# A head's output with tokens on partitions, and attention weights left unnormalised, in a two-layer hybrid decoder trunk

## Chip, cores and metric

One Trainium2 chip, one core, one launch. The metric is the device time of the kernel in microseconds (us). Everything is computed to float32 accuracy: where a matrix product is large, each float32 operand is split into a high and a low part and three products are summed (high x high, high x low, low x high).

## The reference

Two layers over x of 512 tokens by 1024 channels. A layer is a SwiGLU block, a token mixing block and a second SwiGLU block, each behind an RMSNorm with shift, scale and gate from a vector c. The mixing block projects to q, k, v, to the input u of a convolution branch and to two gates. Of its attention branch this matters here:

```
s = einsum('bqhmd,bkhmd->bhmqk', q, k) * scale + bias       # 8 heads, 2 maps (m) each
p = softmax(where(dist >= 0, s, neg))
w = p[:, :, 0] - lam * p[:, :, 1]
o = einsum('bhqk,bkhe->bqhe', w, v)                         # e = 128
o = rms_norm(o, subln_gain) * (1 - lam_init)                # over the 128 channels of a head
y_attn = o.reshape(B, S, 1024) @ w_attn_branch
```

The convolution branch is a gated input (`glu` below), a causal depthwise convolution of width 31, a LayerNorm over channels and a product with a matrix. Since rms_norm divides by sqrt(mean(o^2) + eps), a row of o that is r times too large has the same norm if eps is multiplied by r^2. That identity is what the change uses.

## The kernel before, in words

Activations lie with channels on partitions and the 512 tokens in the free dimension. Every large product is cut into slabs: a weight slab is 1024 x 128, that is 8 blocks of 128x128 (k = 0 to 7). For each slab four steps follow one another. SP loads it (`w_raw`), ACT rounds it to the high part (`w_hi`, `w_hi_part`, L377), DVE subtracts to get the low part (`w_lo`, `w_lo_part`, L605), and PE runs 24 matmuls of 128x512 on it (L1045 to L1047, `slab`). There are two slots of each buffer; the slabs alternate between them, so the `w_hi` of a slab waits until PE has finished the slab two before it, and DVE's `w_lo` waits for that `w_hi`.

The order of every engine is written out by hand; nothing schedules it. In the mixing block one function `mix` per engine handles a head; the first head is written out, the other seven are a loop. A head has six slabs, called slab 0 to 5 here, for q, k, v, the two halves of u, and gate a. The attention work of a head is spread over its own slabs 3 to 5 and over slabs 0 to 2 of the next head:

- PE puts small pieces into slabs by a table `at={k: ...}` (before block k). The scores of the four query blocks (L1222) come at k = 4 of slab 3, behind slab 3, at k = 4 of slab 4 and of slab 5. The weights are turned by transposes (L1198). In the next head, `values` (L1205) follows at k = 4 of slab 1 and `head_mean` (L1210, the mean of the squares over partitions as a product with a constant matrix, L1072) at k = 3 of slab 2.
- DVE interleaves with its `w_lo` parts the 31 taps of the previous head's convolution (`conv`, L858, 0.75 us each), the row maxima (`scores`, L890, and the sign change, L893) and `combine` (L901 to L908), which makes of two exponentials the difference of two softmaxes. It ends a head with `glu` (L944), from which the next 31 taps start. In slabs 1 and 2 of the next head it takes the reciprocal of the root, 128x512 (L616), multiplies o by gain and reciprocal (L627), and later subtracts for `ao_lo` (L634).
- ACT copies results from PSUM, makes the `w_hi` parts and the exponentials (L511), and for the previous head copies o (`head_output`, L499), squares it (L500), takes the root (L384, its table loaded ahead at L381) and rounds the product to `ao_hi` (L396).

Here o comes out of PE with its 128 channels on partitions, so its norm is a sum over partitions, and root and reciprocal stand repeated on all 128 partitions as 128x512.

Behind the loop come gate b (`gb`, four pairs of slabs), the attention projection (`ab`), the convolution projection and the output projection. The last head's rest and 31 taps fall into `gb`; PE's mean over the convolution's sum (L1272) waits for the last tap.

The neighbouring pieces of DVE's program in a head, which the steps of the prediction follow:

```
conv(8, 17)
w_lo_part(p + 1, 1)
if not first:
    reciprocal(...)
    unit_gain(uh, 0, True, OT[:, :], subg[:, ds(l, 1)])
w_lo_part(p + 2, 0)
conv(17, 19)
```

Here `p` counts pairs of slabs: `w_lo_part(p + 1, 1)` is slab 3, `w_lo_part(p + 2, 0)` slab 4, and `w_lo_part(p + 3, 0)` slab 0 of the next head.

Of the kernel before, what the change touches and what calls it, by code (L numbers as in the profile page):

```python
# [27 lines left out]
P = 128  # L28
# [47 lines left out]
AUXN = 3 + HEADS + 2  # L76
AUX_NORM = (0, 1, AUXN - 1)
AUX_HEAD, AUX_MEAN, AUX_VAR = 2, 2 + HEADS, 3 + HEADS

RSN = 3 + HEADS + 1  # L80
RS_NORM = (0, 1, RSN - 1)
RS_HEAD, RS_VAR = 2, 2 + HEADS

UNITS = 3 * KT + HEADS + KT
UNIT_NORM = (0, KT, UNITS - KT)
UNIT_HEAD, UNIT_LN = 2 * KT, 2 * KT + HEADS
# [34 lines left out]
def build(nc, a, onehot, out):  # L121
# [86 lines left out]
    OT = at("o_t", [P, TOK], F32, mr0)  # L208
# [163 lines left out]
    def _(act):  # L372
# [93 lines left out]
        with act.Fori(0, DEPTH) as l:  # L466
            for w in range(2):
# [29 lines left out]
                def head_output(hh):  # L497
                    act.wait_ge(sem("o_ready"), hh + 1)
                    act.activation(OT[:, :], O[:, :], ACT.Copy).then_inc(sem("o_copied"), 1)  # L499
                    act.activation(SQ[:, :], O[:, :], ACT.Square).then_inc(sem("o_read"), 1)  # L500

                def mix(h, first):
# [49 lines left out]
                for j in range(KT):  # L552
# [13 lines left out]
                    if j == 0:  # L566
                        unit_hi(l * UNITS + UNIT_HEAD + HEADS - 1, 0, AOHI[:, HEADS - 1, :])
# [33 lines left out]
    def _(dve):  # L601
# [154 lines left out]
        with dve.Fori(0, DEPTH) as l:  # L756
            for w in range(2):
# [113 lines left out]

                def mix(h, first):
# [3 lines left out]
                    uh = l * UNITS + UNIT_HEAD + h - 1  # L876
# [18 lines left out]
                    def combine(i):  # L895
# [26 lines left out]
                    if not first:  # L922
                        unit_lo(uh, 0, tile(AOLO2, h - 1), tile(AOHI2, h - 1))
# [13 lines left out]
                    combine(0)  # L937
                    if not first:
# [14 lines left out]
                for j in range(KT):  # L953
# [12 lines left out]
                    if j == 0:  # L966
                        uh = l * UNITS + UNIT_HEAD + HEADS - 1
# [360 lines left out]
```

## Time and profile before

| what | value |
|---|---|
| median of 3 runs | 2756.42 us (2755.35 to 2757.57) |
| the profiled execution | 2755.38 us |
| its span, first to last instruction | 2753.7 us |
| mean granted clock of TensorE | 0.978 |
| busy: PE, DVE, ACT | 94%, 63%, 39% of the span |
| traffic with HBM | 319.6 MB, 116 GB/s over the span |

The page gives busy shares over the whole span. Which engine sets the pace of a stage is read from the busy time by stretch and from what each engine waited for in it. A duration in the trace is that of one instruction from start to end; instructions of one engine overlap a little at their ends, so the distance from start to start is the time that one takes in a row of many. "Idle before" is the time from the modelled end of the instruction ahead. The granted clock is 1.00 at 2.4 GHz and 0.50 at 1.2 GHz.

### The profile page before, as it was taken

Reading aid. Unit: us, or ns where it says so; the run is one execution under the profiler, and the core shown is the slowest. Engines: PE = TensorE matmul, PEld = TensorE weight load, DVE = VectorE, ACT = ScalarE, POOL = GpSimd, SP = SyncE. Lnnn points to the kernel's source line nnn. Section 1 sums busy time; section 2 is a strip of 40 time slices with the busy share of each in tenths; the row PEclk is TensorE's granted clock in tenths of the full one; section 3 lists DMA queues with packets and bytes.
Section 4 is the critical chain, followed back from the end, with each engine's and each line's share of the span. In section 5 each row is a group of like instructions: output and inputs, shape, how many; then the busy total and the mean of one; then the engine's idle time right before and its main releaser. Section 6 shows DMA issues by size and latency. Waiting matters only on the chain.

```text
span 2753.7 us, 35127 instructions
## 1 busy us (share of the span) xinstructions
PE 2585.2 (94%) x11186; PEld 2030.9 (74%) x11186; DVE 1748.2 (63%) x2545; ACT 1060.4 (39%) x1497; POOL 81.7 (3%) x162
## 2 busy tenths in 40 slices
PE   4899998999999989999979999989999999899997
PEld 2688886776767767888858888867766678688886
DVE  3655567799998555543345556669999965655433
ACT  2433322444443434343234342244444443443422
POOL 0000010000000000000000001100000000000000
PEclk9999998999999999999989999989999999999998
DMA  5444474222222233433324446622222223343332
GB/s 221 142 149 142 151 224 142 81 76 72 80 80 84 84 114 115 152 122 95 97 83 145 153 129 208 211 66 79 76 73 83 77 87 122 101 143 107 97 92 93
DMA packets 472262, 320.39 MB, mean 116 GB/s; under 512 B 11303, under 2 KB 447785, under 8 KB 471176
## 3 DMA queue, kind: packets, MB, share of 16 engines
q1 hardware_dynamic: 445260, 227.69, 28.1%
q0 software_dynamic: 21888, 83.90, 8.9%
q10 hardware_dynamic: 5052, 8.02, 1.0%
q8 instruction: 33, 0.54, 0.1%
q14 instruction: 29, 0.24, 0.0%
HBM read 314.52 MB, written 5.05 MB: 116 GB/s over the span
## 4 chain that ended last, share of the span: by engine, by line
PE 68%; DVE 16%; issue 11%; ACT 3%; ACTq 1%; DVEq 1%
PE bank L1045 21%; PE bank L1047 21%; PE bank L1046 21%; DVE conv_part L858 5%; DVE rstd L616 3%; DVE w_lo L605 2%; ACTq L420 1%; ACT w_hi L377 1%; DVE probs L890 1%; PE bank L1063 1%; PE bank L1064 1%; PE bank L1065 1%; PE bank L1100 1%; DVE probs L906 1%; PE bank L1127 1%
## 5 line engine op out<-in xcount | busy, mean ns | idle before, releaser
L605 DVE TENSOR_TENSOR w_lo<-w_raw,w_hi 128x1024 fp32r<-128x1024 f32 (+1 forms) x434 | 522.6, 1205 | 721.5 <-ACT w_hi L377 720.6
L1046 PE MATMUL bank<-h_lo,w_hi 128*128 128x512 f32 x2336 | 911.3, 390 | 0.0
L1045 PE MATMUL bank<-h_hi,w_hi 128*128 128x512 f32 x2208 | 885.9, 401 | 17.9 <-DVE w_lo L605 17.8
L1047 PE MATMUL bank<-h_hi,w_lo 128*128 128x512 f32 x2208 | 862.9, 391 | 0.0
L377 ACT ACTIVATE w_hi<-w_raw 128x1024 fp32r<-128x1024 f32 (+1 forms) x434 | 452.4, 1043 | 912.8 <-PE bank L1047 893.1
L1045 PEld LDWEIGHTS bank<-h_hi,w_hi 128*128 128x128 f32 x2208 | 415.5, 188 | 134.9 <-issue 52.2
L1046 PEld LDWEIGHTS bank<-h_lo,w_hi 128*128 128x128 f32 x2336 | 440.1, 188 | 89.9 <-issue 3.8
L1047 PEld LDWEIGHTS bank<-h_hi,w_lo 128*128 128x128 f32 x2208 | 415.4, 188 | 89.0
L858 DVE SCALAR_TENSOR_TENSOR conv_part<-glu,conv_taps,conv_part 128x512 f32<-128x512 f32 x464 | 316.6, 747 | 0.0
L1045 PE MATMUL bank<-s_hi,w_hi 128*128 128x512 f32 x704 | 274.9, 390 | 0.0
L1047 PE MATMUL bank<-s_hi,w_lo 128*128 128x512 f32 x704 | 274.0, 389 | 0.0
L1046 PE MATMUL bank<-s_lo,w_hi 128*128 128x512 f32 x704 | 273.9, 389 | 0.0
L673 DVE SCALAR_TENSOR_TENSOR ada_acc<-ada_raw,c_act,ada_acc 128x1024 f32<-128x1024 f32 x126 | 161.2, 1280 | 0.6
L1045 PEld LDWEIGHTS bank<-s_hi,w_hi 128*128 128x128 f32 x704 | 132.1, 188 | 27.7
L1047 PEld LDWEIGHTS bank<-s_hi,w_lo 128*128 128x128 f32 x704 | 132.1, 188 | 27.6
L1046 PEld LDWEIGHTS bank<-s_lo,w_hi 128*128 128x128 f32 x704 | 132.2, 188 | 27.4
L353 POOL DMA_DIRECT2D ada_raw<-in_ada_w x144 | 76.3, 530 | 2401.5 <-DVE scaled L1006 1065.0
L478 ACT ACTIVATE s_hi<-full 128x512 f32 x88 | 55.7, 633 | 175.0 <-DVE full L779 175.0
L511 ACT ACTIVATE probs<-probs,neg_row_max 128x512 f32<-128x512 f32 (+3 forms) x128 | 71.0, 556 | 115.0 <-DVE neg_row_max L893 114.9
L377 ACT ACT_TABLE_LOAD x88 | 112.9, 1283 | 1.6
L781 DVE TENSOR_TENSOR s_lo<-full,s_hi 128x512 f32 (+1 forms) x88 | 61.0, 693 | 80.3 <-ACT s_hi L478 80.3
L616 DVE RECIPROCAL rstd<-rstd 128x512 f32<-128x512 f32 x25 | 83.7, 3350 | 13.8 <-ACT rstd L384 13.8
(158 smaller groups left out, 2296.5 us busy)
## 6 DMA issues: line engine op xcount, KB each, us to landing
w_raw<-in_ffn_w_in SPq DMA_DIRECT2D x176, 512.0 KB, 3.8
ada_raw<-in_ada_w POOLq DMA_DIRECT2D x144, 512.0 KB, 4.7
w_raw<-in_w_mix_in SPq DMA_DIRECT2D x112, 512.0 KB, 3.7
w_raw<-in_ffn_w_out SPq DMA_DIRECT2D x64, 512.0 KB, 3.6
w_raw<-in_ffn_w_out SPq DMA_DIRECT2D x32, 384.0 KB, 3.1
w_raw<-in_w_mix_out SPq DMA_DIRECT2D x18, 512.0 KB, 3.6
ada_first<-in_ada_w POOLq DMA_DIRECT2D x8, 1024.0 KB, 24.4
w_raw<-in_w_attn_branch SPq DMA_DIRECT2D x16, 512.0 KB, 3.6
```

The costliest lines, as they stand in the source:

```text
L353: pool.dma_start(ada_raw[k % 4][:, :], w_ada[:, ds(layer * KT + k, 1), ds(m * D, D)].rearrange("p o f -> p (o f)"))\
L377: act.activation(whi[slot][:, 0:n, :], raw[slot][:, 0:n, :], ACT.Copy).then_inc(w_hi[slot], 1)
L478: act.activation(tile(SHI2, i), F[0][:, :], ACT.Copy).then_inc(sem("s_hi"), 1)
L511: act.activation(PR[par][m][:, 0:n], PR[par][m][:, 0:n], ACT.Exp, bias=nmx[:, par, m:m + 1], accum_out=rsum[:, par, m:m + 1]).then_inc(sem ...
L605: dve.tensor_tensor(wlo[slot][:, 0:n, :], raw[slot][:, 0:n, :], whi[slot][:, 0:n, :].bitcast(F32), ALU.subtract).then_inc(w_lo[slot], 1)
L616: dve.reciprocal(RSTD[:, :], RSTD[:, :]).then_inc(sem("rstd_ready"), 1)
L673: ins = dve.scalar_tensor_tensor(out=ACC[:, :], in0=ada_raw[k % 4][:, :], scalar=CA[:, k:k + 1], in1=ACC[:, :], op0=ALU.mult, op1=ALU.add)
L781: dve.tensor_tensor(tile(SLO2, i), F[0][:, :], tile(SHI2, i).bitcast(F32), ALU.subtract)\
L858: ins = dve.scalar_tensor_tensor(out=CAB[t % 2][:, :], in0=Z[:, t:t + TOK], scalar=wt, in1=CAB[t % 2][:, :], op0=ALU.mult, op1=ALU.add)
L1045: pe.matmul(acc, wh, hi[:, k0 + k, :], start=first and k == 0, stop=False)
L1046: pe.matmul(acc, wh, lo[:, k0 + k, :], start=False, stop=False)
L1047: mm = pe.matmul(acc, wl, hi[:, k0 + k, :], start=False, stop=last and k == n - 1)
```

## The change

The output of a head is made with tokens on partitions: ten matmuls of 128x128 with the turned weights as the stationary operand, where there were four with V stationary. The sum of squares of a token is then a row sum, which ACT's square gives along with it, and root and reciprocal are 128x4. Four copies with that reciprocal as the scale make the normalised rows, four transposes on PE (`turn_o`) bring the channels back to partitions, and ACT and DVE make `ao_hi` and `ao_lo` from the result with the gain.

The weights are left unnormalised: `combine` forms e0 - lam * (s0 / s1) * e1 (s0, s1 the row sums of the two maps), which is s0 times the former weights. The norm takes this factor out again, with eps * s0^2 as the bias of the root. On DVE the scaling of the second map by its reciprocal (L906) is thus gone.

Places: PE's `head_mean` at k = 3 of slab 2 goes, `turn_o` comes at k = 6 of slab 2. On DVE the small reciprocal stands where the large one stood. On ACT `head_root` stands where `head_output` stood, ahead of the `w_hi` of slab 3, and `head_rows` where `root` stood, ahead of the `w_hi` of slab 4. For the last head `turn_o` comes at k = 2 of slab 0 of gate block 1.

The diff, without tables of counts, declarations and waits of DVE on its own small results (`sum_eps` is called behind `combine(0)`, `head_lo` where `unit_lo` was):

```diff
 ACT
-                def head_output(hh):
+                def head_root(hh):
                     act.wait_ge(sem("o_ready"), hh + 1)
-                    act.activation(OT[:, :], O[:, :], ACT.Copy).then_inc(sem("o_copied"), 1)
-                    act.activation(SQ[:, :], O[:, :], ACT.Square).then_inc(sem("o_read"), 1)
+                    for i in range(QB):
+                        act.activation(SQ[:, i * P:(i + 1) * P], O[:, i * P:(i + 1) * P], ACT.Square,
+                                       accum_out=oss[:, i:i + 1]).then_inc(sem("o_squared"), 1)
+                    act.wait_ge(sem("o_squared"), (hh + 1) * QB)
+                    act.wait_ge(sem("head_eps"), hh + 1)
+                    for i in range(QB):
+                        act.activation(ort[:, i:i + 1], oss[:, i:i + 1], ACT.Sqrt, bias=head_eps[:, i:i + 1],
+                                       scale=1.0 / P).then_inc(sem("o_root"), 1)
+                def head_rows(hh):
+                    act.wait_ge(sem("o_inv"), hh + 1)
+                    act.wait_ge(sem("ot_ready"), hh)
+                    for i in range(QB):
+                        act.activation(OS[:, i * P:(i + 1) * P], O[:, i * P:(i + 1) * P], ACT.Copy,
+                                       scale=ori[:, i:i + 1]).then_inc(sem("o_read"), 1)
+                def head_hi(hh, h):
+                    act.wait_ge(sem("ot_ready"), hh + 1)
+                    act.activation(tile(AOHI2, h), AUX[:, :], ACT.Copy, scale=subg[:, ds(l, 1)]).then_inc(sem("ao_hi"), 1)
...
-                        head_output(hh - 1)
+                        head_root(hh - 1)
                     w_hi_part(p + 1, 1)
                     act.activation(KTT[:, :], G[1][:, :], ACT.Copy).then_inc(acc_read[1], 1)
                     if not first:
-                        root(l * AUXN + AUX_HEAD + h - 1, l * UNITS + UNIT_HEAD + h - 1, float(D // P))
+                        head_rows(hh - 1)
                     w_hi_part(p + 2, 0)
                     act.activation(VT[:, :], G[0][:, :], ACT.Copy).then_inc(acc_read[0], 1)
                     if not first:
-                        unit_hi(l * UNITS + UNIT_HEAD + h - 1, 0, tile(AOHI2, h - 1))
+                        head_hi(hh - 1, h - 1)
 DVE
+                def head_inverse(hh):
+                    dve.wait_ge(sem("o_root"), (hh + 1) * QB)
+                    dve.wait_ge(sem("o_read"), hh * QB)
+                    dve.reciprocal(ori[:, :], ort[:, :]).then_inc(sem("o_inv"), 1)
+                def head_lo(hh, h):
+                    dve.wait_ge(sem("ao_hi"), hh + 1)
+                    dve.scalar_tensor_tensor(out=tile(AOLO2, h), in0=AUX[:, :], scalar=subg[:, ds(l, 1)],
+                                             in1=tile(AOHI2, h).bitcast(F32), op0=ALU.mult, op1=ALU.subtract)
...
-                        dve.reciprocal(rinv[:, par, :], rsum[:, par, :]).then_inc(sem("comb"), 1)
-                        dve.tensor_scalar(rlam[:, par:par + 1], rinv[:, par, 1:2], nlam[:, ds(l, 1)], None, ALU.mult)
-                        dve.tensor_scalar(p1, p1, rlam[:, par:par + 1], None, ALU.mult).then_inc(sem("comb"), 1)
-                        dve.scalar_tensor_tensor(out=p0, in0=p0, scalar=rinv[:, par, 0:1], in1=p1,
+                        dve.reciprocal(rinv[:, i:i + 1], rsum[:, i, 1:2]).then_inc(sem("comb"), 1)
+                        dve.scalar_tensor_tensor(out=ratio[:, i:i + 1], in0=rsum[:, i, 0:1], scalar=nlam[:, ds(l, 1)],
+                                                 in1=rinv[:, i:i + 1], op0=ALU.mult, op1=ALU.mult)
+                        dve.scalar_tensor_tensor(out=p0, in0=p1, scalar=ratio[:, i:i + 1], in1=p0,
                                                  op0=ALU.mult, op1=ALU.add).then_inc(sem("w_ready"), 1)
+                    def sum_eps():
+                        dve.wait_ge(sem("o_root"), hh * QB)
+                        dve.scalar_tensor_tensor(out=head_eps[:, :], in0=rsum[:, :, 0], scalar=EPS, in1=rsum[:, :, 0],
+                                                 op0=ALU.mult, op1=ALU.mult).then_inc(sem("head_eps"), 1)
...
-                        reciprocal(l * AUXN + AUX_HEAD + h - 1, l * RSN + RS_HEAD + h - 1)
-                        unit_gain(uh, 0, True, OT[:, :], subg[:, ds(l, 1)])
+                        head_inverse(hh - 1)
 PE
-                    for j in range(QB):
-                        mm = pe.matmul(O[:, j * P:TOK], V[:, j, :], WT[:, j, j * P:TOK], start=(j == 0), stop=(j == QB - 1))
+                    for i in range(QB):
+                        for j in range(i + 1):
+                            mm = pe.matmul(O[:, i * P:(i + 1) * P], WT[:, j, i * P:(i + 1) * P], V[:, j, :],
+                                           start=(j == 0), stop=(j == i))
...
+                def turn_o(hh):
+                    pe.wait_ge(sem("o_read"), (hh + 1) * QB)
+                    pe.wait_ge(sem("ao_lo"), hh)
+                    for i in range(QB):
+                        mm = pe.transpose(AUX[:, i * P:(i + 1) * P], OS[:, i * P:(i + 1) * P], ident[:, :])
...
-                    slab(p + 1, 0, G[0][:, :], HHI, HLO, at={} if first else {3: lambda: head_mean(h - 1)})
+                    slab(p + 1, 0, G[0][:, :], HHI, HLO, at={} if first else {6: lambda: turn_o(hh - 1)})
...
-                head_mean(HEADS - 1)
+                branch("gb", 1, HHI, HLO, ({2: lambda: turn_o(last)}, {}))
```

How the order of instructions moves, at two places. ACT, inside the head loop, from the turned weights of query block 0 to the first exponential's table; `w_hi_55` is slab 3, `w_hi_54` slab 4. Before:

```order
L493 ACTIVATE weights_t<-bank 128x128
L499 ACTIVATE o_t<-bank 128x512
L500 ACTIVATE squares<-bank 128x512
L377 ACTIVATE w_hi_55<-w_raw_53 128x1024
L522 ACTIVATE k_t<-bank 128x512
L381 ACT_TABLE_LOAD
L381 ACTIVATE root_warm<-eps 128x1
L382 REGISTER_ALU
L383 ISA
L384 ACTIVATE rstd<-bank,eps 128x512
L375 ISA
L377 ACTIVATE w_hi_54<-w_raw_52 128x1024
```

And after the change (L381 is now `w_hi`):

```order
L497 ACTIVATE weights_t<-bank 128x128
L505 ACTIVATE squares,o_square_sum<-bank 128x128 x4
L507 REGISTER_ALU
L510 ACT_TABLE_LOAD
L510 ACTIVATE o_root<-o_square_sum,head_eps 128x1 x4
L381 ACTIVATE w_hi_55<-w_raw_53 128x1024
L546 ACTIVATE k_t<-bank 128x512
L518 ACTIVATE o_rows<-bank,o_root_inv 128x128 x4
L379 ISA
L381 ACTIVATE w_hi_54<-w_raw_52 128x1024
```

The root and its table load have moved ahead of the `w_hi` of slab 3; ahead of the `w_hi` of slab 4 stand the copies that need the reciprocal.

DVE, inside the head loop, from the last of nine taps over `w_lo` of slab 3 to the next two taps. Before:

```order
L605 TENSOR_TENSOR w_lo_57<-w_raw_53,w_hi_55 128x1024
L615 REGISTER_ALU
L616 RECIPROCAL rstd<-rstd 128x512
L617 REGISTER_ALU
L626 ISA
L627 REGISTER_ALU
L627 SCALAR_TENSOR_TENSOR scaled_61<-o_t,subln,rstd 128x512
L604 REGISTER_ALU
L605 TENSOR_TENSOR w_lo_56<-w_raw_52,w_hi_54 128x1024
```

And after the change (L630 is now `w_lo`):

```order
L630 TENSOR_TENSOR w_lo_57<-w_raw_53,w_hi_55 128x1024
L899 ISA
L900 ISA
L901 RECIPROCAL o_root_inv<-o_root 128x4
L629 REGISTER_ALU
L630 TENSOR_TENSOR w_lo_56<-w_raw_52,w_hi_54 128x1024
```

The reciprocal keeps its place between the two `w_lo`, at a 128th of the size, and the multiplication behind it is gone.

## Rows read from the trace of the kernel before

**Rows 1.** The page: the span, and busy time, share and instructions of each engine.
```profile
span 2753.7 us, 35127 instructions
...
PE 2585.2 (94%) x11186; PEld 2030.9 (74%) x11186; DVE 1748.2 (63%) x2545; ACT 1060.4 (39%) x1497; POOL 81.7 (3%) x162
```

**Rows 2.** Busy time by stretch (us and instructions, clock, DMA share, GB/s), one head.
```profile
564.40:608.80 44.40, 42.27 (x185) 30.67 (x184) 42.46 (x84) 20.88 (x40) 0.00 (x0) 1.00 0.27 77
```

**Rows 3.** Timeline of DVE, same head: start us, us, engine, line, operation [idle before].
```profile
562.86 0.69 DVE L944 SCALAR_TENSOR_TENSOR glu<-full,scaled 128x512 f32<-128x512 f32 x1
...
569.86 6.05 DVE L858 SCALAR_TENSOR_TENSOR conv_part<-glu,conv_taps,conv_part 128x512 f32<-128x512 f32 x9
575.83 1.22 DVE L605 TENSOR_TENSOR w_lo<-w_raw,w_hi 128x1024 fp32r<-128x1024 f32 x1
576.96 3.35 DVE L616 RECIPROCAL rstd<-rstd 128x512 f32<-128x512 f32 x1
580.54 0.75 DVE L627 SCALAR_TENSOR_TENSOR scaled<-o_t,subln,rstd 128x512 f32<-128x512 f32 x1 [0.23 <-DVE rstd L616]
581.21 1.22 DVE L605 TENSOR_TENSOR w_lo<-w_raw,w_hi 128x1024 fp32r<-128x1024 f32 x1
...
597.44 1.23 DVE L605 TENSOR_TENSOR w_lo<-w_raw,w_hi 128x1024 fp32r<-128x1024 f32 x1 [0.69 <-ACT w_hi L377]
...
607.33 0.69 DVE L944 SCALAR_TENSOR_TENSOR glu<-full,scaled 128x512 f32<-128x512 f32 x1
```

**Rows 4.** Timeline of PE in the same head, columns as in rows 3.
```profile
570.09 0.47 PE L1045 MATMUL bank<-h_hi,w_hi 128*128 128x512 f32 x1 [0.39 <-DVE w_lo L605]
...
572.25 1.02 PE L1072 MATMUL bank<-squares,inv_d 128*128 128x512 f32 x2
...
573.34 0.39 PE L1046 MATMUL bank<-h_lo,w_hi 128*128 128x512 f32 x1
...
576.33 0.39 PE L1047 MATMUL bank<-h_hi,w_lo 128*128 128x512 f32 x1
...
577.19 0.47 PE L1045 MATMUL bank<-h_hi,w_hi 128*128 128x512 f32 x1 [0.48 <-DVE w_lo L605]
...
585.25 0.92 PE L1222 MATMUL bank<-k_t,q_t 64*128 64x384 f32 x4 [1.03 <-DVE neg_row_max L893]
...
586.09 0.66 PE L1230 MATMUL bank<-ident,v_t 128*128 128x128 f32 x4
...
586.82 0.39 PE L1046 MATMUL bank<-h_lo,w_hi 128*128 128x512 f32 x1
```

**Rows 5.** Groups of instructions over the whole span: count, busy us, mean ns.
```profile
L906 DVE TENSOR_SCALAR probs<-probs,row_inv_lam 128x512 f32<-128x512 f32 (+1 forms) x64 | 24.8, 387 | 2.2
...
L901 DVE RECIPROCAL row_inv<-row_sum 128x2 f32<-128x2 f32 x64 | 10.1, 159 | 0.0
...
L493 ACT ACTIVATE weights_t<-bank 128x128 f32<-128x128 f32 x16 | 4.3, 268 | 0.0
```

**Rows 6.** Timeline of ACT in the same head, columns as in rows 3.
```profile
571.36 1.28 ACT L381 ACT_TABLE_LOAD   x1
...
576.81 1.06 ACT L377 ACTIVATE w_hi<-w_raw 128x1024 fp32r<-128x1024 f32 x1 [2.73 <-PE bank L1047]
```

**Rows 7.** Two idle stretches of PE (timeline), and the clock behind each (by stretch).
```profile
866.12 1.12 PE L1072 MATMUL bank<-running_sum,inv_d 128*128 128x512 f32 x2 [1.79 <-DVE running_sum L870]
...
904.27 0.47 PE L1045 MATMUL bank<-ao_hi,w_hi 128*128 128x512 f32 x1 [3.18 <-DVE gate_a L960]
...
866.20:869.50 3.30, 3.27 (x12) 2.08 (x13) 3.21 (x5) 0.60 (x1) 0.00 (x0) 1.00 0.29 88
...
905.60:908.90 3.30, 3.30 (x10) 2.53 (x9) 1.96 (x4) 2.44 (x4) 0.00 (x0) 0.50 0.82 245
```

**Rows 8.** Timeline of DVE behind the head loop, columns as in rows 3.
```profile
829.64 0.69 DVE L944 SCALAR_TENSOR_TENSOR glu<-full,scaled 128x512 f32<-128x512 f32 x1
...
838.91 1.23 DVE L605 TENSOR_TENSOR w_lo<-w_raw,w_hi 128x1024 fp32r<-128x1024 f32 x1 [4.60 <-ACT w_hi L377]
```

More of the change, by code:

```diff
@@ L73 @@
 USE0, USES = starts(PH_USES)
-AUXN = 3 + HEADS + 2
+AUXN = 5
 AUX_NORM = (0, 1, AUXN - 1)
-AUX_HEAD, AUX_MEAN, AUX_VAR = 2, 2 + HEADS, 3 + HEADS
-RSN = 3 + HEADS + 1
+AUX_MEAN, AUX_VAR = 2, 3
+RSN = 4
 RS_NORM = (0, 1, RSN - 1)
-RS_HEAD, RS_VAR = 2, 2 + HEADS
-UNITS = 3 * KT + HEADS + KT
+RS_VAR = 2
+UNITS = 4 * KT
 UNIT_NORM = (0, KT, UNITS - KT)
-UNIT_HEAD, UNIT_LN = 2 * KT, 2 * KT + HEADS
+UNIT_LN = 2 * KT
 ZERO_FFN1, ZERO_CONV, ZERO_LN, ZERO_MO, ZERO_FFN2, ZEROS = 1, 2, 3, 4, 5, 5
@@ L189, in build @@
     nmx = at("neg_row_max", [P, 2, 2], F32)
-    rsum = at("row_sum", [P, 2, 2], F32)
-    rinv = at("row_inv", [P, 2, 2], F32)
-    rlam = at("row_inv_lam", [P, 2], F32)
+    rsum = at("row_sum", [P, QB, 2], F32)
+    rinv = at("row_inv", [P, QB], F32)
+    ratio = at("row_ratio", [P, QB], F32)
+    head_eps = at("head_eps", [P, QB], F32)
+    oss = at("o_square_sum", [P, QB], F32)
+    ort = at("o_root", [P, QB], F32)
+    ori = at("o_root_inv", [P, QB], F32)
     SHI = at("s_hi", [P, FT, TOK], F32R, r0)
@@ L207, in build @@
     VT = at("v_t", [P, TOK], F32, ph + 4 * KB)
-    OT = at("o_t", [P, TOK], F32, mr0)
+    OS = at("o_rows", [P, TOK], F32, mr0)
     V = at("v", [P, QB, P], F32, ph + 6 * KB)
@@ L560, in _ @@
                         weights(0, l * HEADS + HEADS - 1)
-                        head_output(l * HEADS + HEADS - 1)
-                        root(l * AUXN + AUX_HEAD + HEADS - 1, l * UNITS + UNIT_HEAD + HEADS - 1, float(D // P))
+                        head_root(l * HEADS + HEADS - 1)
                     w_hi_part(p + 1, 1)
@@ L566, in _ @@
                     if j == 0:
-                        unit_hi(l * UNITS + UNIT_HEAD + HEADS - 1, 0, AOHI[:, HEADS - 1, :])
+                        head_rows(l * HEADS + HEADS - 1)
+                    if j == 1:
+                        head_hi(l * HEADS + HEADS - 1, HEADS - 1)
                     if j == LN_MEAN:
@@ L937, in mix @@
                     combine(0)
+                    sum_eps()
                     if not first:
@@ L966, in _ @@
                     if j == 0:
-                        uh = l * UNITS + UNIT_HEAD + HEADS - 1
-                        reciprocal(l * AUXN + AUX_HEAD + HEADS - 1, l * RSN + RS_HEAD + HEADS - 1)
-                        unit_gain(uh, 0, True, OT[:, :], subg[:, ds(l, 1)])
+                        head_inverse(l * HEADS + HEADS - 1)
                         taps(HEADS - 1, 5, 8)
-                        unit_lo(uh, 0, AOLO[:, HEADS - 1, :], AOHI[:, HEADS - 1, :])
                         taps(HEADS - 1, 8, 13)
                     if j == 1:
+                        head_lo(l * HEADS + HEADS - 1, HEADS - 1)
                         taps(HEADS - 1, 22, DVE_TAPS)
@@ L1267, in _ @@
                 branch("gb", 0, HHI, HLO, ({4: lambda: turn_weights(1, last)}, {1: lambda: turn_weights(0, last), 6: lambda: values(last)}))
-                head_mean(HEADS - 1)
-                with pe.Fori(1, LN_MEAN + 1) as i:
+                branch("gb", 1, HHI, HLO, ({2: lambda: turn_o(last)}, {}))
+                with pe.Fori(2, LN_MEAN + 1) as i:
                     branch("gb", i, HHI, HLO)
                 pe.wait_ge(sem("csum"), (l + 1) * KT)
+                pe.wait_ge(sem("ao_lo"), (l + 1) * HEADS)
                 mean(l * AUXN + AUX_MEAN, SSUM[:, :])
@@ L1275, in _ @@
                 with pe.Fori(0, LN_VAR + 1 - KT // 2) as i:
-                    pe.wait_ge(sem("unit_lo"), l * UNITS + UNIT_HEAD + HEADS)
+                    pe.wait_ge(sem("ao_lo"), (l + 1) * HEADS)
                     branch("ab", i, AOHI, AOLO)
```

23 lines of the change are left out of this document (10 added, 13 removed).

## The prediction

> **What bounds the kernel now.** I read the page, then the busy time by stretch, then the timelines of VectorE (DVE), TensorE (PE) and ScalarE (ACT) through one head. The page shows PE busy 94% of the span and DVE 63% [rows 1]. The share is an average over stages. In the head loop, the only stage that the change touches besides the block behind it, DVE is busy 42.46 of 44.40 us and PE 42.27, ACT only 20.88 [rows 2]. From one `glu` to the next is 44.47 us [rows 3]. DVE's idle in it is the 0.69 us shown and some 0.35 behind `glu`. PE, in contrast, has real waits, and all are for DVE: 0.39, 0.48 and 1.03 us of idle [rows 4]. An idle figure counts from the modelled end of a 0.39 us matmul, while matmuls start every 0.23 us (13 starts in the 2.99 us from 573.34 to 576.33 [rows 4]), so each hides 0.16 us more. With two smaller waits that makes 2.8 us, and PE's own work in a head is 41.7 us. DVE sets the period; PE is 2.8 us behind it. A DVE that is faster gives at most 2.8 us a head, unless something new is late.
>
> **What DVE loses and gains per head.** The reciprocal of 128x512 and the wait behind it go, from 576.96 to 580.54: 3.58 us. So does the multiplication by gain and rstd, from 580.54 to 581.21: 0.67 [rows 3]. The four scalings of `probs` go: 4 x 0.387 = 1.55 us [rows 5]. The 128x2 reciprocals and the little product behind them keep their number. Added are a reciprocal of 128x4 and one 128x4 product for `head_eps`; the nearest row is the 128x2 reciprocal, 0.16 each [rows 5]; bounds 0.1 and 0.25, I take 0.16. `ao_lo` stays one 128x512 operation. Net: 3.58 + 0.67 + 1.55 - 0.32 = 5.5 us less work a head, nearly twice what PE could follow.
>
> **Where the new wait is.** Before, the mean of squares was taken at k = 3 of slab 2, and nothing in PE's order waited for DVE's reciprocal. Now PE's `turn_o`, at k = 6 of slab 2, waits for ACT's `head_rows`, and that waits for DVE's `head_inverse`. The latter has kept its place, behind 17 taps and two `w_lo`. Behind the waiting PE instruction are the last six matmuls of slab 2; behind those ACT's `w_hi` of slab 4; behind that DVE's very next instruction, `w_lo` of slab 4. It is a ring. Call the start of the small reciprocal R.
> - Reciprocal 0.16, hand-over 0.05.
> - ACT, four copies of 128x128. One such copy is 0.27 us [rows 5]. One behind another they would be 1.07, and if they overlap by a tenth as long ones do, 0.75. I take 0.8. PE can start at R + 1.05.
> - PE, four transposes. From 586.09 to 586.82 are four transposes and one matmul: 0.73 - 0.23 = 0.50 [rows 4]. Then six matmuls, 1.38, and 0.16 for the tail of the last: R + 3.1.
> - ACT, `w_hi`: it started at 576.81, 0.48 us behind the start of the last matmul (576.33), and took 1.06 [rows 4, 6]. R + 4.25.
>
> DVE, ready at R + 0.2, idles 4.1 us, where before `w_lo` came at once [rows 3]. Two smaller waits follow. `scores(3)` needs PE's slab 3 up to k = 4: R + 1.05, 0.50 and 18 matmuls 4.1, then two score matmuls, 1.2 (the narrower pair at 585.25 took 0.84 [rows 4], times 4/3, and a tail): R + 6.9. DVE is there after `w_lo` 1.13 and two taps (nine take 5.97 us, from 569.86 to 575.83 [rows 3]): R + 6.7. With the hand-over 0.3 us. `w_lo` at 597.44 waited for ACT, which waits for the maxima ahead of `combine(2)`, so what that combine saves, 0.4 us, is lost there. The period is 44.47 - 5.5 + 4.1 + 0.3 + 0.4 = 43.8 us: 0.7 less, over the seven `glu` intervals of a layer 4.9, for two layers **9.8 us less**.
>
> PE's work changes too: mean out, 1.09 - 0.23 = 0.86 (572.25 to 573.34 [rows 4]); transposes in, 0.50; the values in ten matmuls for four, of the same 1280 columns, which I put at 0.1 (bounds 0 and 0.5). That is 41.4 us, so PE waits some 2.4 us at `turn_o`, 2.2 us as the profile counts idle. ACT gains four squares, four roots and four copies. The table load of 1.28 us [rows 6] stood behind `k_t` and ahead of its wait; now it stands behind the squares, ahead of `w_hi` of slab 3. Between the values and `turn_o` lie 30 matmuls, 6.9 us, and the stall, so the values are there at R - 8.2. Squares 1.4 (four at the copy's 0.27 and a tenth more for the sum), load 1.28, roots 0.8, `w_hi` 1.06 and hand-overs 0.2 end at R - 3.5. DVE wants that `w_hi` at R - 1.1: nothing waits, and the cover is 2.4 us.
>
> **What the stall does to PE's clock.** Idle of 1.79 us before 866.12 left the granted clock at 1.00; 3.18 us before 904.27 were followed by 3.3 us at 0.50, that is 1.2 GHz in place of 2.4 [rows 7]. The new stall, 2.2 us, lies between and recurs in every head. In such a stretch PE does 3.3 us of work in twice the time, so loses 1.7 us, and it loses them just where DVE waits for PE (the 0.3 us before `scores(3)`). The cost of a fall is between 0 (where DVE has slack) and 1.7; I take 1.3, near the upper end because the ring lies there. For the number of falls I have only the two rows, so take the middle: half, 7 of 14. That is **+9 us**. The Trainium skill (TensorE: Matmul & The Clock Gate, "HAM oscillation — how this bites in real kernels") describes a loop whose waits let the clock fall again in each pass; by it every head would pay. Its section "What's actually happening" lets the clock fall only after an idle stretch; by that a stall this short would cost nothing. The first is rival B's time, the second rival A's.
>
> **Behind the loop.** Before, from `glu` at 829.64 to the mean at 866.12 are 36.5 us, all DVE, with 4.60 us idle before `w_lo` at 838.91 [rows 7, 8]. Reciprocal and gain go there too, 4.2. But PE now comes later relative to DVE, so DVE idles about 1.1 us more before the first `w_lo` and 1.2 before the second (root and table load ahead of it). `turn_o` in slab 0 of gate block 1 stalls PE 4.4 us, which delays the `w_hi` of block 2 by 1.9. Sum 0. That stall is beyond the 3.18 us, so the clock falls, on this ring: +1.3 a layer, **+2.6 us**. Head 0 and everything else are unchanged.
>
> **Sum.** -9.8 + 9 + 2.6 = +1.8 us on the profiled execution's 2755.38 (span 2753.7 and 1.7 around it), which is 1.0 under the median of the runs. On the median: 2756.4 + 1.8 = 2758. A measurement of this kernel can tell about 0.2%, 5.5 us, from no change.
>
> **Rivals.**
> - A, the clock holds (chance 0.2): the ring as above without falls in the loop. -9.8 + 2.6 = -7: 2749. For it: 2.2 us is nearer to 1.79 than to 3.18.
> - B, slower (0.25): the clock falls in every head, at the full 1.7 us. -9.8 + 14 x 1.7 + 2.6 = +17: 2773. At 1.3 a fall it is +11. It decides from a stall just over 1.79 us, or from copies that cost their upper bound, 0.3 us more a head, 4 us in all.
> - C, no ring (0.05): DVE's relief goes through and PE sets the period, 41.4 us. 14 x 3.1 = 43 us less: 2713. Against it: the order on DVE puts the reciprocal 14 us behind `glu`, and PE is at `turn_o` before that.
> - D, ACT is late (0.05): squares with their sums and the roots cost over 2.4 us more than I count, and `w_hi` of slab 3 holds DVE ahead of the reciprocal. Each further us costs 14: about 2770.
>
> **How the numbers follow.** The forecast, a gain of the loop given back through the clock, has 0.45: 2758, its own range 2751 to 2765. The range over the cases reaches down past A with copies at their lower bound and up to B at the middle of its prices: 2745 to 2771. Faster by over 0.2%: most of A and all of C, 0.25. Slower: B, D and the upper edge of the forecast, 0.32. Within: 0.43.
>
> **What would show it.** In the new profile `turn_o` should be PE's longest wait in a head, 2 to 3 us, released by `o_rows`; the other PE waits in the head nearly gone; DVE idle some 4 us before the `w_lo` behind the 128x4 reciprocal, released by `w_hi`; a `glu` period of 43.8 us where the clock is full and about 45 where it fell. Intervals near 41.4 us would refute the ring. Intervals of 43.8 throughout would be A, of 45 or more throughout B. A wait of DVE before `w_lo` of slab 3 would be D.

## The result, and the profile after

| | this kernel | kernel before |
|---|---|---|
| median | 2781.39 us (2777.96 to 2782.35, 4 runs) | 2756.99 us (2755.35 to 2757.99, 4 runs) |
| profiled execution, its span | 2777.96, 2776.2 us | 2755.38, 2753.7 us |
| mean granted clock | 0.970 | 0.978 |

The ratio is 1.0087, 95% interval 1.0071 to 1.0103: slower by 24 us, where 2758 (2745 to 2771) was forecast. The profiled execution was the fastest of the four and is 22.5 us longer in its span than that of before.

The page answers to [rows 1]: DVE is busy for 81 us less, PE for nearly the same (2.3 us more).

```profile
span 2776.2 us, 35599 instructions
...
PE 2587.5 (93%) x11410; PEld 2062.8 (74%) x11410; DVE 1667.3 (60%) x2481; ACT 1077.8 (39%) x1689; POOL 81.4 (3%) x162
```

Busy time by stretch (as [rows 2]), two heads from one `glu` to the next:

```profile
609.00:653.50 44.50, 41.05 (x200) 31.73 (x199) 37.44 (x80) 21.96 (x52) 0.00 (x0) 1.00 0.26 76
653.50:699.70 46.20, 42.75 (x201) 32.92 (x199) 37.50 (x81) 21.98 (x52) 0.00 (x0) 0.96 0.26 74
```

In the first the clock was full: 44.5 us, DVE busy for 37.44 where it was 42.46. The head is no shorter. In the second the granted clock was 0.96 on average and the head took 46.18 us, 1.6 us more.

DVE's timeline in the first of these heads answers to [rows 3]; the bracket is the idle before and what ended it:

```profile
608.96 0.69 DVE L985 SCALAR_TENSOR_TENSOR glu<-full,scaled 128x512 f32<-128x512 f32 x1
...
621.92 1.23 DVE L630 TENSOR_TENSOR w_lo<-w_raw,w_hi 128x1024 fp32r<-128x1024 f32 x1
623.06 0.18 DVE L901 RECIPROCAL o_root_inv<-o_root 128x4 f32<-128x4 f32 x1
627.70 1.23 DVE L630 TENSOR_TENSOR w_lo<-w_raw,w_hi 128x1024 fp32r<-128x1024 f32 x1 [4.46 <-ACT w_hi L381]
...
630.36 0.69 DVE L927 CUSTOM_DVE_ANT_0 probs<-bank,bias_tile 128x512 f32<-128x512 f32 x1
...
643.66 1.23 DVE L630 TENSOR_TENSOR w_lo<-w_raw,w_hi 128x1024 fp32r<-128x1024 f32 x1 [1.14 <-ACT w_hi L381]
...
646.68 0.06 DVE L925 MEMSET spare<- 128x1 f32 x1 [0.47 <-PE bank L1237]
...
653.51 0.69 DVE L985 SCALAR_TENSOR_TENSOR glu<-full,scaled 128x512 f32<-128x512 f32 x1
```

The large reciprocal (3.35 us) has become 0.18 us, and the `w_lo` behind it, which used to come at once, waits 4.46 us. Two waits stand later in the head: 1.14 us before the `w_lo` of slab 0 (0.69 before), and 0.47 us ahead of `scores(0)`, for the turned weights, where there was none. Before `scores(3)` there is hardly a wait: its first instruction starts at 630.36, 0.1 us behind the two taps. From `glu` to `glu` are 653.51 - 608.96 = 44.55 us, against 44.47.

ACT and PE at the place of the ring, as [rows 6] and [rows 4]. ACT:

```profile
615.40 1.28 ACT L510 ACT_TABLE_LOAD   x1
616.70 0.85 ACT L510 ACTIVATE o_root<-o_square_sum,head_eps 128x1 f32<-128x1 f32 x4
617.46 1.04 ACT L381 ACTIVATE w_hi<-w_raw 128x1024 fp32r<-128x1024 f32 x1
...
623.27 1.14 ACT L518 ACTIVATE o_rows<-bank,o_root_inv 128x128 f32<-128x128 f32 x4 [4.29 <-DVE o_root_inv L901]
626.60 1.06 ACT L381 ACTIVATE w_hi<-w_raw 128x1024 fp32r<-128x1024 f32 x1 [2.19 <-PE bank L1086]
```

PE, the last matmul before the transposes, the transposes, and a matmul behind them:

```profile
620.63 0.39 PE L1086 MATMUL bank<-h_hi,w_lo 128*128 128x512 f32 x1
624.47 0.66 PE L1254 MATMUL bank<-ident,o_rows 128*128 128x128 f32 x4 [3.45 <-ACT o_rows L518]
...
625.19 0.39 PE L1085 MATMUL bank<-h_lo,w_hi 128*128 128x512 f32 x1
```

Here the ring can be followed. The reciprocal starts at 623.06, the four copies at 623.27 take 1.14 us, PE's transposes start at 624.47 after 3.45 us of idle, the last six matmuls of slab 2 follow, `w_hi` starts at 626.60, and DVE's `w_lo` at 627.70: 4.64 us from the reciprocal, of which DVE worked 0.2. ACT, in contrast, had its `w_hi` of slab 3 done at 618.50, 3.4 us before DVE wanted it: the roots and their table load delayed nothing.

What the stall does to the clock is seen one head earlier. PE:

```profile
578.43 1.11 PE L1254 MATMUL bank<-ident,o_rows 128*128 128x128 f32 x4 [3.45 <-ACT o_rows L518]
579.20 0.78 PE L1084 MATMUL bank<-h_hi,w_hi 128*128 128x512 f32 x1
579.77 0.63 PE L1085 MATMUL bank<-h_lo,w_hi 128*128 128x512 f32 x1
580.20 0.63 PE L1086 MATMUL bank<-h_hi,w_lo 128*128 128x512 f32 x1
```

and the stretch behind the stall:

```profile
578.30:581.50 3.20, 3.07 (x10) 2.59 (x11) 0.00 (x0) 0.08 (x1) 0.00 (x0) 0.50 0.55 164
```

The granted clock was 0.50, and matmuls start every 0.43 us (579.77, 580.20) instead of every 0.23. In that head DVE waits longer for the `w_hi`:

```profile
583.14 1.23 DVE L630 TENSOR_TENSOR w_lo<-w_raw,w_hi 128x1024 fp32r<-128x1024 f32 x1 [5.94 <-ACT w_hi L381]
```

In the loop the clock fell in 11 of 14 heads; those take 45.9 to 46.2 us, the others 44.55. In six of the eleven the low stretch begins up to 0.5 us before the transposes, and this wait is 5.81 to 5.94 us instead of 4.46. In the other five it begins some 1.8 us later; the wait is 4.85 to 4.93 us, and the one before `scores(3)` has grown from 0.1 to 1.26 to 1.32 us.

DVE behind the loop, answering to [rows 8]:

```profile
837.74 0.69 DVE L985 SCALAR_TENSOR_TENSOR glu<-full,scaled 128x512 f32<-128x512 f32 x1
839.02 1.23 DVE L630 TENSOR_TENSOR w_lo<-w_raw,w_hi 128x1024 fp32r<-128x1024 f32 x1 [0.59 <-ACT w_hi L381]
...
848.68 1.22 DVE L630 TENSOR_TENSOR w_lo<-w_raw,w_hi 128x1024 fp32r<-128x1024 f32 x1 [5.60 <-ACT w_hi L381]
...
859.03 1.23 DVE L630 TENSOR_TENSOR w_lo<-w_raw,w_hi 128x1024 fp32r<-128x1024 f32 x1 [3.76 <-ACT w_hi L381]
...
874.81 0.69 DVE L895 TENSOR_TENSOR running_sum<-running_sum,conv 128x512 f32<-128x512 f32 x1
```

The wait for `w_hi` is 5.60 us instead of 4.60, and two others have come, 0.59 and 3.76. They eat what the reciprocal gave. PE's stall at `turn_o` is 4.55 us there, and the clock falls in both layers, for 3.4 and 6.8 us. It fell there in the kernel before as well, for as long, behind a wait of PE for `w_lo`:

```profile
851.55 0.77 PE L1045 MATMUL bank<-h_hi,w_hi 128*128 128x512 f32 x1 [3.54 <-DVE w_lo L605]
```

But from there to the mean DVE waited for no other engine, so that fall did not delay it; now DVE waits for the `w_hi` behind it. The wait of 3.76 us is 4.52 in the other layer, where the clock was low for longer.

**Where the 22.5 us are** (profiled executions, by the starts of `glu` and of the means on PE). The seven intervals of a layer took 311.3 us; now 319.4 and 320.9, together 17.7 more. Without falls they would be 7 x 44.55 = 311.9, so 1.2 us belong to the head as it is at full clock and 16.5 to the clock, 1.5 us for each of the eleven falls. From the last `glu` to the mean 36.5 us have become 37.9 and 38.6 (38.65): 3.6. The rest, 1.2 us, lies elsewhere; its cause was not looked for.

### The profile page after: what moved, and what is told of

Read it like the earlier page. It is cut to its first block, busy times and chain, and to the rows that moved or that the text cites. A ratio compares the mean times of both kernels' runs of the same rounds, so it can differ in the third digit from the quotient of the medians.

```text
span 2776.2 us, 35599 instructions
## 1 busy us (share of the span) xinstructions
PE 2587.5 (93%) x11410; PEld 2062.8 (74%) x11410; DVE 1667.3 (60%) x2481; ACT 1077.8 (39%) x1689; POOL 81.4 (3%) x162
## 4 chain that ended last, share of the span: by engine, by line
PE 80%; DVE 9%; issue 7%; ACT 3%; ACTq 1%; DVEq 1%
PE bank L1084 24%; PE bank L1085 24%; PE bank L1086 24%; DVE conv_part L883 3%; PE bank L1267 2%; DVE w_lo L630 1%; ACTq L424 1%; DVE rstd L641 1%; PE bank L1102 1%; PE bank L1103 1%; PE bank L1104 1%; ACT w_hi L381 1%; PE bank L1139 1%; ACT o_rows L518 1%; PE bank L1254 1%
## 5 line engine op out<-in xcount | busy, mean ns | idle before, releaser
L630 DVE TENSOR_TENSOR w_lo<-w_raw,w_hi 128x1024 fp32r<-128x1024 f32 (+1 forms) x434 | 522.8, 1205 | 815.1 <-ACT w_hi L381 814.2
L1084 PE MATMUL bank<-h_hi,w_hi 128*128 128x512 f32 x2208 | 884.0, 400 | 0.1
L381 ACT ACTIVATE w_hi<-w_raw 128x1024 fp32r<-128x1024 f32 (+1 forms) x434 | 452.1, 1042 | 897.5 <-PE bank L1086 877.8
L1102 PE MATMUL bank<-h_hi,w_hi 128*128 128x512 f32 x96 | 47.9, 499 | 46.7 <-DVE h_lo L661 46.7
```

The source lines that it names most:

```text
L381: act.activation(whi[slot][:, 0:n, :], raw[slot][:, 0:n, :], ACT.Copy).then_inc(w_hi[slot], 1)
L630: dve.tensor_tensor(wlo[slot][:, 0:n, :], raw[slot][:, 0:n, :], whi[slot][:, 0:n, :].bitcast(F32), ALU.subtract).then_inc(w_lo[slot], 1)
L1084: pe.matmul(acc, wh, hi[:, k0 + k, :], start=first and k == 0, stop=False)
L1102: pe.matmul(acc, wh, hi[:, n, :], start=n == 0, stop=False)
```

## The experiments

The theory after this reading: in a head DVE's relief is given back through a ring (reciprocal, copies, `turn_o`, end of slab 2, `w_hi`, `w_lo`), and the PE stall in it makes the clock fall, 1.5 us each time. The rivals: the added instructions cost the time, or the long heads have another cause and the clock only follows.

A block is three matmuls. All medians are beside runs of the kernel before, which gave 2754.65 us in the first four experiments and 2755.88 in the others.

### e1: `turn_o` in slab 3

```diff
-slab(p + 1, 0, ..., at={} if first else {6: lambda: turn_o(hh - 1)})
+slab(p + 1, 0, ...)
-slab(p + 1, 1, ..., at={4: lambda: scores(3)})
+slab(p + 1, 1, ..., at={4: lambda: scores(3)} if first else {3: lambda: turn_o(hh - 1), 4: lambda: scores(3)})
-branch("gb", 1, HHI, HLO, ({2: lambda: turn_o(last)}, {}))
+branch("gb", 1, HHI, HLO, ({}, {3: lambda: turn_o(last)}))
```

> Theory (a ring through PE's wait at turn_o): with turn_o at k = 3 of slab 3 the w_hi and w_lo of slab 4 no longer hang on DVE's reciprocal. DVE's idle of 4.5 us before the w_lo behind it goes; about 2 us come back before scores(3), which needs slab 3 of PE. Period of a head 41.5 to 42.3 us, no fall of the clock in the loop, 2712 to 2725 us. Rival (the added instructions themselves cost the time: ten value matmuls for four, four squares, roots and copies on ACT): nothing is left out here, so it stays within 5 us of 2781.

Measured: 2717.9 us median, ratio 0.9864 (0.9848 to 0.9881). A head takes 42.03 us, the first of a layer 42.70, no fall in the loop. The same instructions in another place are 63 us faster than the change and 37 faster than before. The added work is thus not the cause; the place of one wait is. Of the ring's wait, 4.46 us, this is left (those of 1.14 and 0.47 us later in the head stay):

```profile
661.62 1.23 DVE L630 TENSOR_TENSOR w_lo<-w_raw,w_hi 128x1024 fp32r<-128x1024 f32 x1 [2.16 <-ACT w_hi L381]
```

2.16 us: slab 2 ends later than DVE is ready, but no longer on account of the reciprocal. I had expected the 2 us before `scores(3)`; no wait shows there, so the period came out right with the wait in another place. Behind the loop, where `turn_o` moved too, 34.0 us are left of the 37.9 and 38.6.

### e2: the stall filled

```diff
                 def turn_o(hh):
+                    pe.wait_ge(sem("ao_lo"), hh)
+                    for _ in range(3):
+                        pe.matmul(AUX[:, :], invd[:, :], X[:, 0, :], start=True, stop=True)
                     pe.wait_ge(sem("o_read"), (hh + 1) * QB)
-                    pe.wait_ge(sem("ao_lo"), hh)
```

> The change with three mean-sized matmuls (0.86 us each, results overwritten by the transposes) put into PE's stall before turn_o, so that PE is at work there; the ring stays as it is. Theory (each fall of the clock costs about 1.5 us, eleven in the loop): all heads take 44.5 to 44.7 us, 2781 - 16 = 2763 to 2767 us. Rival (the 46 us heads are long for another reason, and the clock falls in them as a consequence): no gain, 2780 or above, since work was only added.

Measured: 2758.99 us median, ratio 1.0014 (1.0005 to 1.0024), 4 us below the expected range. PE in a head (the three matmuls are six records):

```profile
621.00 2.74 PE L1253 MATMUL bank<-x_res,inv_d 128*128 128x512 f32 x6
624.60 0.66 PE L1256 MATMUL bank<-ident,o_rows 128*128 128x128 f32 x4 [0.86 <-ACT o_rows L518]
```

The filling lasts 2.74 us and 0.86 us of idle are left. No fall in the loop, and twelve of the fourteen intervals are 44.51 to 44.55 us (the first of each layer 45.29, since there the stall was short and the filling costs). Work was added and 22 us went: the falls are the cause of the long heads, not their consequence. The ring is unchanged (DVE waits 4.46 us in it, as in the change), and a head is still 0.05 us longer than one of before, so the kernel is no faster than before either. The profiled executions differ by 16.8 us in span (2759.4): 15.3 in the loop, that is eleven falls at 1.5 less what the filling costs in the two first heads, and 2.0 behind it, where the filling stands too, which I had not counted (elsewhere e2 takes 0.5 more). There one layer had a fall and took 38.06 us, the other had none and took 36.45, as long as before the change. The medians differ by 5.6 us more than the spans, since the profiled execution of the change was 3.4 us under its median and that of e2 2.2 over it.

### e3: the reciprocal earlier

```diff
-                    conv(8, 17)
-                    w_lo_part(p + 1, 1)
+                    conv(8, 12)
                     if not first:
                         head_inverse(hh - 1)
+                    conv(12, 17)
+                    w_lo_part(p + 1, 1)
```

> The small reciprocal moved up by five taps and one w_lo on DVE, everything else as in the change. Theory (ring): the rows are there before PE reaches turn_o at k = 6 of slab 2, no stall, no fall; period 41.3 to 42.2 us, 2710 to 2723 us. If instead ACT's root is not ready so early, DVE waits before the reciprocal, and the gain is halved. Rival (added work): within 5 us of 2781.

Measured: 2723.19 us median, ratio 0.9887 (0.9870 to 0.9903), at the upper end of the expected range. A head takes 41.64 us. The ring is opened at its other end, with nearly the same effect. PE no longer waits at `turn_o`; its one wait of the head is for the low part of slab 3:

```profile
660.40 0.47 PE L1085 MATMUL bank<-h_hi,w_hi 128*128 128x512 f32 x1 [0.51 <-DVE w_lo L630]
```

Behind the loop `turn_o` still stalls for 4.5 us; the two stretches there take 38.0 and 39.2 us against 34.0 in e1. That is why e1, 4.5 us slower in the loop, is faster in all.

### e4: `turn_o` one block later

```diff
-slab(p + 1, 0, ..., at={} if first else {6: lambda: turn_o(hh - 1)})
+slab(p + 1, 0, ..., at={} if first else {7: lambda: turn_o(hh - 1)})
```

> turn_o one block (three matmuls, 0.69 us) later in slab 2. Theory (ring): the ring holds three matmuls of slab 2 instead of six, so a head without a fall takes 44.55 - 0.69 = 43.9 us; PE's stall shrinks to some 3 us but the clock still falls in most heads, at 1.5 us. 14 x 0.69 = 10 us less: 2769 to 2773 us. Rival (the place of turn_o is indifferent, DVE's own work sets the head): 2781.

Measured: 2759.65 us median (2756.76 to 2770.74, 10 runs), ratio 1.0024 (1.0012 to 1.0036). Heads without a fall take 43.84 to 43.87 us, 0.69 less, which is the three matmuls (3 x 0.23). PE's idle in most heads:

```profile
580.64 0.66 PE L1254 MATMUL bank<-ident,o_rows 128*128 128x128 f32 x4 [2.76 <-ACT o_rows L518]
```

The miss is in the number of falls: I expected most heads, and the profiled execution had only 4 in 14. Seven falls fewer than in the change, at 1.5 us, are 10.5 us. They bring the theory's 2771 us down to 2760.5, near the measured time, which is 9 us below the expected range. Only the profiled execution shows its falls; the ten runs lie 14 us apart.

### e5: the weights part alone, on the kernel before

Without waits and counts:

```diff
-                        dve.reciprocal(rinv[:, par, :], rsum[:, par, :])
-                        dve.tensor_scalar(rlam[...], rinv[:, par, 1:2], nlam[:, ds(l, 1)], None, ALU.mult)
-                        dve.tensor_scalar(p1, p1, rlam[:, par:par + 1], None, ALU.mult)
-                        dve.scalar_tensor_tensor(out=p0, in0=p0, scalar=rinv[:, par, 0:1], in1=p1, ...)
+                        dve.reciprocal(rinv[:, par, 1:2], rsum[:, par, 1:2])
+                        dve.scalar_tensor_tensor(out=rlam[...], in0=rsum[:, par, 0:1], scalar=nlam[:, ds(l, 1)],
+                                                 in1=rinv[:, par, 1:2], op0=ALU.mult, op1=ALU.mult)
+                        dve.scalar_tensor_tensor(out=p0, in0=p1, scalar=rlam[:, par:par + 1], in1=p0, ...)
```

> The kernel before with only the weights left unnormalised (the scaling L906 gone); eps of the head's norm is left unscaled. Theory (before, DVE sets the head, and the place ahead of the w_lo of slab 0, where DVE waits for ACT anyway, swallows 0.4 us): 44.47 - 1.7 + 0.4 = 43.1 to 43.4 us a head, 15 to 19 us less than before: 2737 to 2741 us. Rival (PE or ACT carries the head as much as DVE): no change, 2755.

Measured: 2739.27 us median, ratio 0.9943 (0.9927 to 0.9958), a head 43.23 us. This half of the change is a gain of 17 us. DVE:

```profile
604.68 0.68 DVE L942 SCALAR_TENSOR_TENSOR glu<-full,scaled 128x512 f32<-128x512 f32 x1
...
638.72 1.23 DVE L605 TENSOR_TENSOR w_lo<-w_raw,w_hi 128x1024 fp32r<-128x1024 f32 x1 [1.14 <-ACT w_hi L377]
...
647.90 0.68 DVE L942 SCALAR_TENSOR_TENSOR glu<-full,scaled 128x512 f32<-128x512 f32 x1
```

The wait before this `w_lo` has grown from 0.69 to 1.14 us, as in the changed kernel: 0.45 of the saving is swallowed there. PE followed DVE down to 43.23 us, so DVE did set the head before.

### e7: the output part alone

`combine` is as in the kernel before (L901 to L908). Besides:

```diff
-                    act.wait_ge(sem("head_eps"), hh + 1)
...
-                        act.activation(ort[:, i:i + 1], oss[:, i:i + 1], ACT.Sqrt, bias=head_eps[:, i:i + 1],
+                        act.activation(ort[:, i:i + 1], oss[:, i:i + 1], ACT.Sqrt, bias=eps[:, 0:1],
...
-                    sum_eps()
```

> The change with the weights normalised as before (L906 back) and a constant eps: the new head output alone. Theory (DVE's work is part of the ring with the stall): some 1 us of the 1.7 comes on top in each head, 45.4 to 45.7 us without a fall, and PE's longer stall lets the clock fall in nearly all: 2790 to 2800 us. Rival (the ring is made of hand-overs only, DVE's work is beside it): 2781.

Measured: 2801.86 us median, ratio 1.0171 (1.0156 to 1.0187), 2 us above the expected range. Heads are 47.6 to 48.0 us (46.78 once), the first of a layer 45.2, and the clock fell in 12 of 14. This half costs 46 us. DVE in a head with a fall:

```profile
632.80 1.22 DVE L630 TENSOR_TENSOR w_lo<-w_raw,w_hi 128x1024 fp32r<-128x1024 f32 x1 [6.09 <-ACT w_hi L382]
...
636.54 0.69 DVE L927 CUSTOM_DVE_ANT_0 probs<-bank,bias_tile 128x512 f32<-128x512 f32 x1 [1.19 <-issue]
...
650.35 1.23 DVE L630 TENSOR_TENSOR w_lo<-w_raw,w_hi 128x1024 fp32r<-128x1024 f32 x1 [0.69 <-ACT w_hi L382]
```

DVE waits 6.09 us behind the reciprocal, and 1.19 before the scores. I had counted 1.5 us for a fall; here 11 of the 12 low stretches lasted 6.8 us instead of 3.4. What a fall of that length costs is read from e4 and e8, which have heads without one: 2.7 to 2.8 us, against 1.3 to 1.7 for one of 3.4. That a head without a fall would take 45.4 to 45.7 us stays open, as every head but the first of a layer had one.

### e8: one copy for four

```diff
-                    for i in range(QB):
-                        act.activation(OS[:, i * P:(i + 1) * P], O[:, i * P:(i + 1) * P], ACT.Copy,
-                                       scale=ori[:, i:i + 1]).then_inc(sem("o_read"), 1)
+                    act.activation(OS[:, :], O[:, :], ACT.Copy).then_inc(sem("o_read"), QB)
```

> The change with the four scaled copies of 128x128 replaced by one unscaled copy of 128x512, waiting for the reciprocal as before; the head's normalisation by the root is left out. Theory (the copies, 1.14 us, stand in the ring; one copy takes 0.60): 0.54 us less a head, 44.0 us without a fall, and a few falls less: 2765 to 2773 us. Rival (they do not matter): 2781.

Measured: 2768.44 us median, ratio 1.0039 (1.0023 to 1.0054). ACT and PE in a head:

```profile
578.23 0.60 ACT L517 ACTIVATE o_rows<-bank 128x512 f32<-128x512 f32 x1 [4.33 <-issue]
```

```profile
578.88 0.65 PE L1252 MATMUL bank<-ident,o_rows 128*128 128x128 f32 x4 [2.94 <-ACT o_rows L517]
```

One copy of 0.60 us in place of 1.14, and a head without a fall takes 44.02 to 44.06 us: 0.5 us less, so the copies stand in the ring at their full length. The clock fell in 8 of 14 heads; four of these take 45.66 to 45.70 us (low for 3.4 us), four 46.77 to 46.82 (low for 6.8).

### e6: both ends opened

```diff
-                    conv(8, 17)
-                    w_lo_part(p + 1, 1)
+                    conv(8, 12)
                     if not first:
                         head_inverse(hh - 1)
+                    conv(12, 15)
+                    w_lo_part(p + 1, 1)
+                    conv(15, 17)
...
-branch("gb", 1, HHI, HLO, ({2: lambda: turn_o(last)}, {}))
+branch("gb", 1, HHI, HLO, ({}, {3: lambda: turn_o(last)}))
```

> The change with the small reciprocal five taps and the w_lo of slab 3 two taps earlier on DVE, and for the last head turn_o at k = 3 of slab 1 of gate block 1. Theory: with the early reciprocal alone PE still waited 0.7 us a head, for the w_lo of slab 3; that goes, and a head takes PE's own work, 41.0 us. With the 4 us a layer that the later turn_o saved behind the loop: 2703 to 2712 us. Rival (PE does not go below 41.6 whatever DVE does): 2715.

Measured: 2705.80 us median (2703.10 to 2707.16, 5 runs), ratio 0.9816 (0.9803 to 0.9829): 50 us faster than before and 76 faster than the change. Both halves of the change are whole in it; two calls have moved on DVE and one on PE. Between two `glu`:

```profile
644.23 0.69 DVE L987 SCALAR_TENSOR_TENSOR glu<-full,scaled 128x512 f32<-128x512 f32 x1
...
685.09 0.68 DVE L987 SCALAR_TENSOR_TENSOR glu<-full,scaled 128x512 f32<-128x512 f32 x1
```

40.86 us (42.75 in the first of a layer), and in the loop PE has nothing left to wait for:

```profile
640.00:681.00 41.00, 41.00 (x201) 31.95 (x200) 37.59 (x80) 21.99 (x53) 0.00 (x0) 1.00 0.29 85
```

PE busy 41.00 of 41.00 us. With this the head is PE's, and by this trace a still faster DVE should bring nothing; no run tries it.

## Why the prediction was wrong

**What bounds before.** Right. DVE set the head: with 1.7 us less of its work alone the period fell by 1.24 (e5). PE's own work after the change is 40.9 us (e6), where I had 41.4; C's floor was thus half a microsecond too high.

**The gain of the loop without falls: the step that failed most.** Forecast 9.8 us less, measured 1.2 more. The ring is right as a mechanism and in its place; each link is in the trace, and moving either end removes the stall (e1, e3). Its length was not. I had DVE ready at R + 0.2 and released at R + 4.25; it was R + 4.64. The term mis-sized was ACT's four copies. Between the bounds 0.75 and 1.07 I took 0.8; they took 1.14, more than the upper bound. The overlap was as assumed (four in 1.14 us at 0.37 each), but the row I took the duration from was a copy without a scale ([rows 5], 0.27 us), and one with a scale per partition takes 0.1 us more. The groups of instructions of this kernel have it:

```profile
L518 ACT ACTIVATE o_rows<-bank,o_root_inv 128x128 f32<-128x128 f32 x64 | 18.3, 369 | 56.4 <-DVE o_root_inv L901 56.4
```

That is 0.34 us a head, and e8 confirms that the copies count in full.

**A wait that the prediction does not list.** Before `scores(0)` DVE waits for the turn of the weights of block 2, which is at k = 6 of slab 5: 0.47 us in every head, and in no head of before. It is not the stall's doing: it stands as well in e6, where PE has no stall, and it is missing in e7, which has the stall, and in e5. It takes both halves of the change; by what path was not followed.

Of the waits that the prediction lists, the one before `scores(3)` is 0.1 us, not 0.3, and the relief of DVE is 5.4 us from start to start, not 5.5. The period adds up as 44.47 - 5.4 + 4.46 + 0.11 + 0.45 + 0.47 = 44.56, against 44.55 measured.

**The clock.** Here the step that failed is the forecast's middle between two rows: "half, 7 of 14" at an idle of 2.2 us. The idle was 3.45 us, because the period was 0.75 longer and PE's work 0.5 shorter than I had them. By then it lay above the 3.18 us that [rows 7] show to be followed by a fall. There were 11 falls at 1.5 us, 16.5 us in place of 9. The price, between 0 and 1.7 and taken as 1.3, was near. (The 1.7 is what a stretch of 3.3 us at half the clock leaves undone; "3.3 us of work in twice the time" is worded wrongly.) Its place was not: I had the loss before `scores(3)` alone, and in six of the eleven heads nearly all of it, in the others about a quarter, is in the wait for `w_hi` of slab 4. So the forecast was wrong to give B hardly more than A: what the sum of the ring could leave out was a further wait or a longer link, and both make the stall longer.

**Behind the loop.** Forecast +2.6, measured +3.6. The sum of 0 without a fall is what the layer of e2 without one shows (36.45 us against 36.48), and a fall there costs 1.4 and 2.2 us by the two layers of the change against it. That the single terms cancel is in part luck: the wait before the first `w_lo` is 0.59 us where I had 1.1. I overlooked that the clock fell there before the change too; that the new fall counts in full rests on DVE now waiting behind it.

**The rivals.** B, a fall in every head at the full price, 2773 us, is the nearest to what came: a fall in all but three of the 14 heads (the first of each layer and one more), at 1.5 us. The measured time is 8 above it. The ring's gain that did not come is worth 11 us more than B has, the falls 7.3 less; the rest is the end of the loop, elsewhere, and 2.4 us by which the medians lie further apart than the profiled executions. D did not occur: `w_hi` of slab 3 had 3.4 us to spare. The sum by terms, forecast and measured in the profiled execution: loop without falls -9.8 and +1.2, falls +9 and +16.5, behind the loop +2.6 and +3.6, elsewhere 0 and +1.2; in all +1.8 and +22.5.

The clock fell in 11 of the 12 heads with a stall of 3.45 us, nearly in each pass of the loop. The Trainium skill (TensorE: Matmul & The Clock Gate, "HAM oscillation — how this bites in real kernels") describes this for a loop that waits 3 to 5 us for DMA in each pass; the trace agrees. For a stall of the 2.2 us that was forecast it does not say so; "by it every head would pay" read too much into it. Stalls of 2.75 to 2.79 us were followed by a fall in 4 of 12 heads (e4). By the Trainium skill's section "What's actually happening" (the same title), as the prediction reads it, a stall that short would cost nothing, which was rival A; the measurement speaks against it at these lengths, and no run here has a stall of 2.2 us.

## What to carry to other kernels

When a slow instruction on the pacing engine goes, ask what it stood in front of. If another engine now waits for the short instruction in its place, and the pacing engine's next operand comes from behind that wait, the time returns as idle; either end can be moved (the producer ahead of work that nobody waits for, the waiting instruction behind the work that somebody waits for), and here each turned 24 us of loss into over 30 of gain. A stall of TensorE that recurs can be charged twice, once as itself and once through the clock: here it was in some heads from 2.75 us of idle on, and never up to 1.9. When the length of such a ring is a sum of small links taken from single instructions, round every link up before comparing it with a limit.

## What was not expected of the hardware

**Falls of the clock against the idle ahead of `turn_o`**, heads of the loop in the profiled executions, one of each kernel; the idle as the profile gives it, and how many of the falls lasted 6.8 us (the others 3.4):

| kernel | idle, us | heads with a fall | of these 6.8 us |
|---|---|---|---|
| first heads of a layer in the change, e4, e8 and e7 | 0.90 to 1.89 | 0 of 8 | |
| e4 | 2.75 to 2.79 | 4 of 12 | 1 |
| e8 | 2.94 to 2.98 | 8 of 12 | 4 |
| the change | 3.44 to 3.48 | 11 of 12 | 0 |
| e7 | 3.90 to 3.95 | 12 of 12 | 11 |

The same stall in the same program sometimes trips the clock and sometimes not, and the share rises within 1.2 us from a third to all. A forecast for such a stall has to be a chance, not a yes or no. What decides it in a head, and how long the clock stays low, was not tested: the change has the longer stall but no fall of 6.8 us, e8 the shorter and four.

**Small operations on ACT.** A copy of 128x128 from PSUM takes 0.37 us with a scale per partition and 0.27 without. Four roots of 128x1 took 0.85 us in all, with a column as the bias. The table load of 1.28 us was followed at once by the root (615.40 and 616.70).
